# Halved last scatter, transposes by column halves, and moved modulation sums in a fused block kernel

## What is computed

```python
def reference(...):
    x = first_block(...)      # one hybrid layer
    return second_block(...)  # two layers

# end of the first block
x = x + routed_experts(rmsnorm(x, g_ffn), ...)   # top 4 of 32 experts
hp = rmsnorm(x, g_ple)
x = x + jax.nn.sigmoid(hp @ w_ple_gate) * (p_i @ w_ple_proj)

# one layer of the second block
mod = c_act @ w_ada[l] + b_ada[l]
shift, scale, gate = jnp.split(mod, 3, axis=-1)
h = rms_norm(x, g_pre[l]) * (1.0 + scale) + shift
proj = h @ w_in[l]            # u_a, b_a, c_a, gate_a, u_p, gate_p
...
x = x + gate * rms_norm(y, g_post[l])
```

## Time and profile before

| | |
|---|---|
| median of 3 runs | 1376.56 us (1375.72 to 1377.74) |
| profiled execution | 1376.27 us |
| its span | 1374.5 us |
| mean granted clock of TensorE | 0.984 |
| TensorE matmul busy | 1319.8 us, 96% |
| VectorE busy | 498.5 us, 36% |
| ScalarE busy | 313.0 us, 23% |

### The profile page before, as it was taken

How to read it: one execution, slowest core, us unless ns; L and a number is a source line. 1 busy time by engine, 2 the same in 40 slices (tenths; PEclk the granted TensorE clock), 3 DMA queues, 4 the chain that set the end, 5 groups by cost and what they waited for, 6 DMA issues and landing times.

```text
span 1374.5 us, 16474 instructions
## 1 busy us (share of the span) xinstructions
PE 1319.8 (96%) x6734; PEld 698.0 (51%) x6734; DVE 498.5 (36%) x742; ACT 313.0 (23%) x435; POOL 55.2 (4%) x70
## 2 busy tenths in 40 slices
PE   9999999999999989989998998989989999999998
PEld 6656686433343334333333333334333346998997
DVE  3676474222222112221222112212221227876764
ACT  4376653101011001010101001001010115632631
POOL 2113110000000000000000000000000001000000
PEclk9999999999999999999999999999999999999999
DMA  9998677999999999999999999999999998446430
GB/s 331 387 327 292 238 301 310 417 429 436 429 428 435 424 435 431 432 429 427 435 425 437 429 429 432 427 434 432 429 432 428 436 420 306 153 169 210 158 125 31
DMA packets 69215, 498.74 MB, mean 363 GB/s; under 512 B 6247, under 2 KB 7738, under 8 KB 51770
## 3 DMA queue, kind: packets, MB, share of 16 engines
q1 hardware_dynamic: 68042, 496.06, 87.7%
q0 software_dynamic: 704, 2.10, 0.5%
q10 hardware_dynamic: 432, 0.07, 0.0%
HBM read 497.06 MB, written 1.05 MB: 362 GB/s over the span
## 4 chain that ended last, share of the span: by engine, by line
PE 69%; DMA 26%; DVE 2%; ACT 1%; issue 1%; SPq 1%; POOL 0%; DVEq 0%; POOLq 0%; ACTq 0%
PE ps L1977 32%; DMA ring<-in_w_gate_up_dram 25%; PE ps L1683 5%; PE ps L1685 5%; PE ps L1684 5%; PE ps L1971 4%; PE ps L1965 3%; PE ps L1717 2%; PE ps L1711 2%; PE ps L1712 2%; PE ps L1727 2%; PE ps L2185 1%; PE ps L2099 1%; PE ps L1981 1%; DMA ring<-in_w_in_dram 1%
## 5 line engine op out<-in xcount | busy, mean ns | idle before, releaser
L1977 PE MATMUL ps<-ring,arena 128*64 128x512 f32 x2304 | 527.4, 612 | 40.6 <-DMA ring<-in_w_gate_up_dram 40.6
L1977 PEld LDWEIGHTS ps<-ring,arena 128*64 128x64 f32 x2304 | 163.7, 140 | 366.5 <-issue 321.2
L1977 PE MATMUL ps<-arena 128*64 128x512 f32 x768 | 170.1, 595 | 1.5 <-issue 1.5
L1394 DVE TENSOR_SCALAR arena<-ps 128x512 f32<-128x512 f32 x32 | 22.1, 692 | 342.5 <-PE ps L1977 342.5
L849 ACT ACTIVATE arena<-arena 128x512 f32<-128x512 f32 x32 | 20.2, 630 | 425.8 <-DVE arena L1394 425.8
L1977 PEld LDWEIGHTS ps<-arena 128*64 128x64 f32 x768 | 53.9, 137 | 105.8 <-issue 104.7
L1368 DVE TENSOR_TENSOR X<-X,ps 128x1024 f32<-128x1024 f32 x34 | 41.4, 1218 | 169.8 <-PE ps L1971 169.8
L1685 PE MATMUL ps<-arena_highs,w_low 128*128 128x256 f32 x320 | 89.8, 281 | 0.0
L1373 DVE COPY arena<-ps 64x512 f32<-64x512 f32 x32 | 22.0, 689 | 170.8 <-PE ps L1977 170.8
L858 ACT COPY arena<-ps 64x512 f32<-64x512 f32 x32 | 18.5, 579 | 232.9 <-PE ps L1977 232.9
L1971 PE MATMUL ps<-arena 128*128 128x512 f32 x136 | 67.1, 617 | 0.0
(11 more groups left out here) (318 smaller groups left out, 1572.6 us busy)
## 6 DMA issues: line engine op xcount, KB each, us to landing
ring<-in_w_gate_up_dram SPq DMA_DIRECT2D x42, 4096.0 KB, 30.4
ring<-in_w_down_dram SPq DMA_DIRECT2D x48, 2048.0 KB, 29.0
arena<-in_w_gate_up_dram SPq DMA_DIRECT2D x14, 4096.0 KB, 31.3
ring<-in_w_in_dram SPq DMA_DIRECT2D x37, 1024.0 KB, 7.2
arena<-in_w_down_dram SPq DMA_DIRECT2D x16, 2048.0 KB, 29.7
ring<-in_w_ada_dram SPq DMA_DIRECT2D x24, 1024.0 KB, 14.1
ring<-in_w_gate_up_dram SPq DMA_DIRECT2D x12, 2048.0 KB, 11.8
ring<-in_w_out_dram SPq DMA_DIRECT2D x12, 1024.0 KB, 5.7
```

The lines of the kernel that those rows point to most:

```text
L1977: last = T.matmul(ps[at:at + CAP, bank, :], lhsT, w(g), start=False, stop=stop)
```

## The change

The last scatter is issued as four matmuls in the order half 0 and half 1 of columns 0 to 511, then both of columns 512 to 1023, each with its own count; VectorE adds in four pieces of 512 columns. The transposes follow by pair: both halves of "hT0", the embedding term, both halves of "hT1". `mod_sums` moves from before the gate to the start of the second block, where the filler matmul stood in the first layer (it stays in the second), and writes bank 7. `mod_columns(1, ...)` moves on VectorE from the gate's columns to behind the low part of chunk 9. TensorE waits for it before group 1 instead of before gate group 1. The low part of chunk 5 moves on VectorE from the end of the gate into the columns of the first layer, between the first pair's lows and the second pair's whole columns.

```diff
+        LAST_PAIR = [3, 0]
+        MOD1_BANK = 7
...
-            for h in range(HALVES):
-                add_scattered(extra * E + (E + h), h, 0 if h else 3)
+            for u in range(2 * HALVES):
+                h, at = u % 2, slice(u // 2 * 512, u // 2 * 512 + 512)
+                dve.wait_ge(s["sc_ready"], extra * E + (E + u + 1))
+                V.tensor_tensor(X[:, h, at], X[:, h, at], ps[:, 2 * LAST_PAIR[h] + u // 2, :], ALU.add
+                                ).then_inc(s["sc_used"], 1)
...
             def before_lows(j):
-                if not j:
-                    dve.wait_ge(s["mod1_full"], 1)
-                    mod_columns(1, 5, s["mod1_moved"], 1)
                 w_split(j)
...
-                w_split(4 + g)
+                if not g:
+                    w_split(4)
...
                 columns(full_of, moved_of,
                         lambda o, a, i: V.tensor_scalar(o, a, cols(mods_f, 24 * l + 8 + i), cols(mods_f, 24 * l + i),
-                                                        ALU.mult, ALU.add), HT, HT_r, lambda j: None)
+                                                        ALU.mult, ALU.add), HT, HT_r,
+                        lambda j: w_split(5) if l == 0 and j else None)
                 for m in range(2, 6):
                     w_split(m0 + m)
+                if l == 0:
+                    dve.wait_ge(s["mod1_full"], 1)
+                    mod_columns(1, MOD1_BANK, s["mod1_moved"], 1)
...
-            scatter(0)
             pe.wait_ge(s["gu_used"], extra * E + (E + FIRST))
-            scatter(1, 0)
-            for h in range(HALVES):
-                pe.wait_ge(s["sc_used"], extra * E + (E + 1 + h + FIRST))
-                for k in range(KC):
-                    p = U3[f"hT{k // 4}"][0]
-                    last = T.transpose(flat(p, P, k % 4 * S + h * P), X[:, h, k * P:k * P + P], ident)
-                    if h and k % 4 == 3:
-                        last.then_inc(full3[p], 1)
-                if not h:
+            for g in range(2):
+                for h in range(HALVES):
+                    T.matmul(ps[:, 2 * LAST_PAIR[h] + g, :], scat[:, h, g, :], yslot[g], start=True, stop=True
+                             ).then_inc(s["sc_ready"], 1)
+            for g in range(2):
+                pe.wait_ge(s["sc_used"], extra * E + (E + 2 * g + 2 + FIRST))
+                p = U3[f"hT{g}"][0]
+                for h in range(HALVES):
+                    for k in range(4):
+                        at = g * 512 + k * P
+                        last = T.transpose(flat(p, P, k * S + h * P), X[:, h, at:at + P], ident)
+                last.then_inc(full3[p], 1)
+                if not g:
                     embedding_term(3, 1, pT_last).then_inc(s["p_full"], 1)
-            mod_sums(1, 5, s["mod1_full"])
...
-            pe.wait_ge(s["mod1_moved"], 1)
             pe.wait_ge(s["p_moved"], 1 + len(EMB))
...
-                keep_busy(2 * lfree("hT1"), 1)
                 if l:
+                    keep_busy(2 * lfree("hT1"), 1)
                     spread_gains()
                     normed_columns(0)
                 else:
+                    mod_sums(1, MOD1_BANK, s["mod1_full"])
                     normed_columns(0)
                     spread_gains()
...
                 for i in range(3):
+                    if l == 0 and i == 1:
+                        pe.wait_ge(s["mod1_moved"], 1)
                     group(i)
```

## The result

The changed kernel takes 1382.82 us (1381.88 to 1383.62, 6 runs) against 1376.14 us for the kernel before in the same set; the ratio is 1.0045 with a 95% interval of 1.0035 to 1.0055. It is slower by 6.7 us, where 6.0 was forecast. The profiled execution has a span of 1380.8 us, 6.3 more than before, at a mean granted clock of 0.981.

What follows compares the result with a forecast made beforehand. TensorE was taken to bound the kernel after the expert loop. A 3.7 us later group 1 plus 2.3 us for the fallen clock made 6.0 us, added to the median 1376.56: 1382.6 us, range 1379.5 to 1384.8.

Steps and rivals of the forecast that it cites:

- What bounds: After the expert loop TensorE sets the end, so a delay put in front of it there comes out undiminished.
- The gate, 0.8 us: First block's gate ends 0.8 us sooner, bounds 0.5 to 1.0, as VectorE's chain is shorter.
- The sums for the filler, 0.15 us: Second block's start: modulation sums of 1.0 us replace 0.86 us of filler, losing 0.15 us.
- Group 0, 1.6 us sooner: Second block: group 0 starts near 1175.8 instead of 1177.41, as VectorE starts its columns sooner.
- The new wait, 3.7 us: Group 1 waits for VectorE's read of bank 7, starting about 1192.5 instead of 1188.83, after 5.3 us idle.
- The clock, 2.3 us: Behind the gap before group 1 TensorE's matmuls run slow, costing 2.3 us, bounds 0 and 3.0.
- the estimate that went with it: Behind the gap, 4.6 us at the low clock level would hold 21.6 matmuls and cost 2.0 us.
- The sum: Whole kernel: 3.7 + 2.3 = 6.0 us slower, added to the median 1376.56, gives 1382.6 us.
- The clock did fall: Rival at the gap before group 1: the clock holds, only the 3.7 us stand, 1380.3; chance 0.10.
- The wait was not covered: Rival at group 1: the new wait is covered, group 1 starts 0.9 us sooner, 1375.7; chance 0.12.
- The halves did not lose anything: Rival at the gate: the halves win nothing, the 0.8 us fall away, 6.8 us slower, 1383.4; chance 0.08.

Runs made afterwards that it cites:

- the single runs: Column halves alone on the kernel before, 1376.50 us; and the changed kernel with the read early and last scatter, sum and transposes as whole halves of tokens, 1376.54 us.

## Why the prediction was right

**What bounds.** Right: everything behind group 1 is shifted by a constant. Its distance to the end is 185.67 us before, and 185.73 with five fillers, 185.75 with the read early.

**The gate, 0.8 us.** Right in size: the start of its last 56 matmuls came 0.85 us sooner (16.96 behind the mark instead of 17.81), its end 0.73. The prediction's 0.8 holds 0.5 for the modulation operations and so 0.3 for the halves; the single runs show 0.1 and 0.4, and the rest only when both are there, since with the halves alone the read waits for the sums.

**The sums for the filler, 0.15 us.** Right: 1.0 us (1168.94 to 1169.94) for 0.86.

**Group 0, 1.6 us sooner.** Mis-sized: 1.15 us. VectorE's columns started where expected (35.8 us behind the mark for 35.7), but TensorE waited for ScalarE's, which started at 1174.71 and released it at 1176.00:

```profile
1174.71 1.95 ACT L887 ACTIVATE arena_highs<-ps,mods 128x256 fp32r<-128x256 f32 x4
```

It made the gap 4.79 us instead of 5.3 and cost nothing at the end, since group 1 did not wait for group 0.

**The new wait, 3.7 us.** Right: 3.82 (53.59 less 49.77). VectorE was done with chunk 9 at 53.4 us behind the mark, for 53.2 computed.

**The clock, 2.3 us.** Right in kind, low by 0.4. Group 1's first 27 matmuls took 5.91 us (1192.39 to 1198.30), where 27 x 0.118 = 3.2 would do: 2.7. So the price did carry over to matmuls of another kind, which the prediction had left open. Its 2.3 is a slip: the three prices of the earlier trace rows are 2.7, 1.7 and 3.0, of which the middle is 2.7; 2.3 is the midpoint of the smallest and the largest. The five gaps that are not shown there fit: in that trace the four of 2.98 to 3.58 us cost 1.5 to 1.7, the four of 3.77 to 4.38 cost 2.3 to 3.0. The Trainium skill, page "TensorE: Matmul & The Clock Gate", section "Back-to-back issue gap", spaces matmuls at the low level by columns over 1.2 GHz, 213 ns for 256 columns; the trace agrees, with 5.34 us for 25 steps, 214 ns each. What was off in the estimate that went with it is how long the low level lasts behind group 1's start: 5.8 us, not 4.6.

**The sum.** 3.82 + 2.74 = 6.56 behind the mark, where 3.7 + 2.3 = 6.0 was said; the expert part of this execution ended 0.26 us sooner, hence 6.3 in span. That the median, 1382.82, is so near to the 1382.6 forecast is in part luck: the sum was 0.6 low, and the median of the kernel before is 0.4 lower in the larger set (1376.14 for 1376.56).

**The rivals.** The clock did fall. The wait was not covered, for the reason named: five low parts stood ahead in a queue in order. The halves did not lose anything: alone they won 0.1 us.

## What to carry to other kernels

A tiny read that frees a buffer must be placed by what stands ahead of it in its engine's queue, not by when its data is ready or by its own length: here 0.18 us of work, ready 22 us early, cost 6.6 us. When it is moved, look for the engine's idle time (1.56 us on VectorE just ahead), and check that nothing else has been moved into the same hole, as happened in the run with the read early and chunk 5 back. Count a gap on TensorE of some microseconds twice, once for itself and once for the slow matmuls behind it, which here cost 1.6 to 2.7 us behind gaps of 2.80 us and more; five filler products took the second away, not the first.

## What the runs showed of the hardware that was not expected

The price of the fallen clock does not simply grow with the idle time. Idle times of 2.80 and 3.10 us cost 1.6 us, 4.79 cost 2.7 (twice), and 10.83 cost 1.7. Nor does the clock have to fall in the gap: at 2.80 and 3.10 us it fell when TensorE was at work again.

No length of gap divides what costs from what does not in these traces. In the expert loop of the kernel before, a gap of 2.57 us cost nothing, while 2.80 us here did cost; but in the expert loop of the run with the read behind the pooling sums a gap of 2.30 us (before 442.78) was followed by a clock of 0.50 and 32 matmuls in 8.78 us, not 7.09. Each of these is one execution.
